# Paired attention scores, pipelined compressed attention and rope rows by DMA in a two-block float32 kernel

## The chip, the core and the metric

One core of a Trainium2 chip runs the whole program. The metric is the time of one execution on the device in microseconds. A kernel is timed in several executions, of which the median counts; one more execution is recorded by the hardware profiler, and all rows below are from it.

## What is computed

Two transformer blocks on 256 tokens of width 2048, all in float32. The first one mixes a selective-scan part (SSD) and sparse attention (NSA), then a gated feed-forward. The second mixes HGRN2 and FOX, then a feed-forward.

```python
# block 1, attention: 16 query heads of 64 in 4 key groups
q_rot = partial_rope(q, cos, sin); ks = partial_rope(ks, cos, sin); kw = partial_rope(kw, cos, sin)
k_cmp = compress_tokens(kc, ...)        # 15 compressed keys and values of 32 tokens each
o_cmp = softmax(q . k_cmp, masked) @ v_cmp
o_sel = softmax(q_rot . ks) @ vs        # n_select covers all 4 blocks: causal attention
o_win = softmax(q_rot . kw) @ vw        # the window covers all 256 tokens
o = g0 * o_cmp + g1 * o_sel + g2 * o_win
# partial_rope: of each head's 64 features, the first 8 (x1) and the next 8 (x2)
x1 * c - x2 * s, x2 * c + x1 * s
# block 2
y_a = hgrn2(q, f, i, g) @ w_up_a;  y_b = fox(q, k, v, f) @ w_up_b
x = x + rms_norm((sigmoid(g_a) * y_a + sigmoid(g_b) * y_b) @ w_o)
x = x + rms_norm((silu(h @ gate) * (h @ up)) @ w_down)
```

## The kernel before

All weights stream through once. `plan` cuts them into items (`1k`, `1q0`, `2ga3` and so on, a chunk of up to 512 output columns each) and items into units of 512 KB. SP loads unit j into one of five `raw` buffers as soon as VectorE has split unit j-5. ScalarE rounds it to `whi` (L992), VectorE takes the rest `wlo` (L1493), and TensorE multiplies three times per weight tile, whi with xhi, whi with xlo, wlo with xhi, for nearly the precision of float32. A "feat" unit is 24 matmuls of 256 moving columns, a "tok" unit 12 of 512. The units of `1mk` and `1mv` (kind "cmp", the compression weights) have only 8 matmuls. The splits run three units ahead of TensorE.

The order is written by hand. On each engine `walk` goes through the items; after each unit it calls `tick()` for short generators and then takes one step, up to its next `yield`, of a side generator: attention, compressed attention, SSD, HGRN, FOX. So the side work of the four engines moves in steps, one a unit, and a `yield` more or less on one engine shifts it by a unit against the others. Matmuls go through L411, transposes through L415.

What the change touches:
- Rope (`rope`, L652 and L1833). Six matmuls with a permutation matrix `perm` bring feature d+8 to d and back, for 2 pairs of key tiles beside `1q1` and 4 pairs of query tiles beside `1v`; VectorE multiplies by cos and sin and adds.
- Attention (`attention1`, `attend`). 24 tasks (`T1`): a task holds 4 heads for the first 128 tokens and 2 heads for the other 128, one key group `g`, one branch. Key group g lies in partitions 0 to 63 for even g and 64 to 127 for odd g, so a score matmul uses one half of the array. Task j: TensorE's scores in step j, VectorE's scaling and masking in j+1, ScalarE's exponential in j+2, TensorE's transposes of the probabilities in j+3, ScalarE's copy of them in j+4, TensorE's value products in j+4 too, VectorE's normalising `fin` in j+5. The steps lie beside `1c`, `1x0`, `1mk`, `1mv` and the start of `1x1`. Banks 4 to 7 of PSUM are handed out in turn by `take` and `give`; a `take` waits for what last read the bank.
- `taps(n)`: the convolution over four tokens of `1x0` to `1x2`, on VectorE and ScalarE, started right behind each item.
- Compressed attention (`compressed`): after the 24 tasks, one token block after the other, in one set of buffers. Its score matmuls alternate between the array's halves and two banks.
- HGRN (`hgrn`): nine levels for two groups of heads, three steps a level: score matmuls, ScalarE's exponential of differences, VectorE's predicated copy of the scores and its products `QE`, `KE` (factors) for the next level.
- `o_tiles`: transposes of the mixers' result, split into the operand of `2ua` and `2ub`. The first two pairs of tiles come right ahead of `2ua0`.
- `between_2fg0`: transposes of quads of the hidden state between the units of the first feed-forward item of block 2.

Of the kernel before, what the change touches and what calls it, by code (L numbers as in the profile page):

```python
# [6 lines left out]
P = 128  # L7
# [13 lines left out]
_CONST = [("w2k", 256), ("w2v", 128), ("ident", 128), ("U", 128), ("OS", 256), ("perm", 128), ("cm", 256), ("lev", 1024),  # L21
# [100 lines left out]
def build(nc, ins, out):  # L122
# [13 lines left out]
    with ctx:  # L136
# [80 lines left out]
        PT1 = [W_(18512, 512), W_(19024, 512)]  # L217
        RT = W_(20048, 512)
        hidT = W_(19536, 2, 256)
# [56 lines left out]
        t16a = small(16)  # L276
        sp = [small(32) for _ in range(4)]
# [20 lines left out]
        s_rope_mm, s_rope_out, s_rope = sem("s_rope_mm"), sem("s_rope_out"), sem("s_rope")  # L298
# [94 lines left out]
        def tensor(e):  # L393
# [234 lines left out]
            def hidden_T(nm):  # L628

                yield from later(2)  # L630
                kv = int(nm == "1mv")
                pb = take("hT", kv)
# [19 lines left out]
            def rope(src, n0, ntile, ready):  # L652
                for i in range(ntile // 2):
                    if i:
                        give("rope", n0 + i - 1, when=(s_rope_out, n0 + i))
                    pb = take("rope", n0 + i)
                    on.wait_ge(*ready)
                    mm(pb, C("perm"), src[:, 2 * i:2 * i + 2, :].rearrange("p a b -> p (a b)")).then_inc(s_rope_mm, 1)
                    yield
                give("rope", n0 + ntile // 2 - 1, when=(s_rope_out, n0 + ntile // 2))  # L660
                yield

            def attend(lab, n, base, outs, PM, PT, scores, values):

                for i in range(n + 5):
# [4 lines left out]
                    if 5 <= i and outs[i - 5][2]:  # L670
                        give(lab, "out", outs[i - 5][0], when=(s_fin, outs[i - 5][0] + 1))
                    if 4 <= i < n + 4:
                        j = i - 4
# [11 lines left out]
                    if i < n:  # L685
                        scores(i, take(lab, "sc", i)).then_inc(s_sc, 1)
                    yield

            def attention1():
# [3 lines left out]
                def scores(j, pb):  # L693
                    tb, hh, br, g, r0, nh, _, _ = T1[j]
                    Kn, p0 = 128 * (tb + 1), (g % 2) * 64
# [20 lines left out]
                yield from attend("a1", N1, 0, outs, PM1, PT1, scores, values)  # L716

            def compressed():
                yield
                w2k, w2v = two(C("w2k")), two(C("w2v"))  # L720
                pb = take("kc")
                on.wait_ge(s_hs, 1)
                for ht in range(2):
                    m = mm(pb[:, 0:60], w2k[:, ht, :], hid[:, 0, ht, :], start=(ht == 0), stop=(ht == 1))
                m.then_inc(s_kc, 1)
                give("kc", when=(s_kcT, 1))
                for gp in range(2):
                    pb = take("vb", gp)
                    on.wait_ge(s_hrep, 1)
                    for ht in range(2):  # L730
# [1744 lines left out]
```

## Time and profile before

| | us |
|---|---|
| median of three timed executions | 2665.29 (2656.59 to 2667.74) |
| the profiled execution | 2660.39 |
| its span in the trace | 2658.6 |
| TensorE busy | 2639.5 |
| VectorE, ScalarE busy | 1482.0, 1239.3 |
| mean granted clock of TensorE | 0.998 |

TensorE is the engine that sets the time; the others are idle for about half of it on average, but not in each stretch. A matmul's shown length reaches to its modelled end, and its successor starts before that. So the difference of two starts tells what a piece costs, and idle time is only shown where the next start lies behind the modelled end. Float32 matmuls that are not split by hand (attention, rope) show as two records each.

### The profile page before, as it was taken

The page shows a single profiled execution, that of the slowest core. Times are in us where ns is not written, and L with a number is a line of the kernel's source. Part 1 is how long each engine was busy: PE and PEld are TensorE (multiplying, and loading weights), DVE is VectorE, ACT ScalarE, POOL GpSimd, SP SyncE. Part 2 cuts the span into 40 slices and gives each one's busy share as a digit, 9 for nine tenths or more (in the row PEclk, how much of TensorE's full clock was granted, in tenths as well). Part 3 has the DMA queues.
Part 4 walks back from the last instruction along what each step waited for, and adds up shares of the span by engine and source line. Part 5 has one row for each costly group of instructions (what it writes and reads, how often), then busy time and mean ns, then how long its engine had stood idle before and what let it go on. Part 6 is the DMA issues. An engine that isn't in the chain of part 4 may idle for free.

```text
span 2658.6 us, 33234 instructions
## 1 busy us (share of the span) xinstructions
PE 2639.5 (99%) x13682; PEld 2250.4 (85%) x13682; DVE 1482.0 (56%) x1790; ACT 1239.3 (47%) x1577; POOL 0.2 (0%) x4
## 2 busy tenths in 40 slices
PE   9999999999999999999999999999999999999998
PEld 9898878888888888889889888888888888888887
DVE  6575776455445454566567654456555444555456
ACT  5465555444344434466454454444554444443443
POOL 0000000000000000000000000000000000000000
PEclk9999999999999999999999999999999999999999
DMA  8433445655555555556544445665555555655554
GB/s 300 151 105 120 151 137 193 200 188 192 192 190 189 191 194 192 188 176 218 189 156 146 154 134 182 193 226 182 184 199 195 185 194 189 194 189 191 191 193 145
DMA packets 131911, 483.64 MB, mean 182 GB/s; under 512 B 14640, under 2 KB 14896, under 8 KB 130736
## 3 DMA queue, kind: packets, MB, share of 16 engines
q1 hardware_dynamic: 131616, 481.37, 55.2%
q8 instruction: 108, 1.77, 0.3%
q14 instruction: 43, 0.35, 0.0%
q10 hardware_dynamic: 144, 0.15, 0.0%
HBM read 477.27 MB, written 4.19 MB: 181 GB/s over the span
## 4 chain that ended last, share of the span: by engine, by line
PE 97%; DVE 1%; DMA 1%; ACT 1%; issue 0%; SPq 0%; DVEq 0%; ACTq 0%
PE ps L411 95%; PE ps L415 2%; DMA h<-in_x 0%; DVE wlo L1493 0%; DMA raw<-in_w_in 0%; ACT W L992 0%; DVE xlo L1496 0%; DVE h L1496 0%; ACT whi L992 0%; DVE W L1493 0%; ACT xhi L992 0%; DVE hlo L1496 0%; DVE scr L1493 0%; SPq L2304 0%; ACT L992 0%
## 5 line engine op out<-in xcount | busy, mean ns | idle before, releaser
L1493 DVE TENSOR_TENSOR wlo<-raw,whi 128x1024 fp32r<-128x1024 f32 x886 | 1082.4, 1224 | 1031.9 <-ACT whi L992 1028.2
L992 ACT ACTIVATE whi<-raw 128x1024 fp32r<-128x1024 f32 x886 | 935.3, 1058 | 1144.9 <-PE ps L411 1133.6
L411 PE MATMUL ps<-whi,xlo 128*128 128x512 f32 x2080 | 817.6, 393 | 1.8 <-DVE xlo L1496 1.8
L411 PE MATMUL ps<-wlo,xhi 128*128 128x512 f32 x2080 | 809.9, 389 | 0.0
L411 PE MATMUL ps<-whi,xhi 128*128 128x512 f32 x2080 | 809.6, 389 | 0.0
L411 PEld LDWEIGHTS ps<-whi,xlo 128*128 128x128 f32 x2080 | 390.6, 188 | 82.4 <-issue 3.5
L411 PEld LDWEIGHTS ps<-wlo,xhi 128*128 128x128 f32 x2080 | 390.4, 188 | 81.9
L411 PEld LDWEIGHTS ps<-whi,xhi 128*128 128x128 f32 x2080 | 390.7, 188 | 80.6 <-issue 1.4
L411 PE MATMUL ps<-whi,hlo 128*128 128x512 f32 x944 | 370.1, 392 | 0.0
L411 PE MATMUL ps<-wlo,hhi 128*128 128x512 f32 x944 | 367.5, 389 | 0.0
L411 PE MATMUL ps<-whi,hhi 128*128 128x512 f32 x944 | 367.3, 389 | 0.0
L411 PE MATMUL ps<-xhi,whi 128*128 128x256 f32 (+2 forms) x992 | 284.7, 288 | 0.7 <-ACT xhi L992 0.4
L411 PE MATMUL ps<-xhi,wlo 128*128 128x256 f32 (+2 forms) x992 | 279.4, 283 | 0.6 <-DVE wlo L1493 0.6
L411 PE MATMUL ps<-xlo,whi 128*128 128x256 f32 (+2 forms) x992 | 279.3, 283 | 0.0
L411 PEld LDWEIGHTS ps<-wlo,hhi 128*128 128x128 f32 x944 | 177.2, 188 | 37.0
L411 PEld LDWEIGHTS ps<-whi,hhi 128*128 128x128 f32 x944 | 177.3, 188 | 36.6 <-issue 0.5
L411 PEld LDWEIGHTS ps<-whi,hlo 128*128 128x128 f32 x944 | 177.2, 188 | 36.4 <-issue 0.5
L411 PEld LDWEIGHTS ps<-xhi,whi 128*128 128x128 f32 (+2 forms) x992 | 187.0, 189 | 6.2 <-issue 4.6
L411 PEld LDWEIGHTS ps<-xlo,whi 128*128 128x128 f32 (+2 forms) x992 | 187.2, 189 | 1.6 <-issue 1.0
L411 PEld LDWEIGHTS ps<-xhi,wlo 128*128 128x128 f32 (+2 forms) x992 | 187.0, 189 | 1.2 <-DVE wlo L1493 0.8
L411 PE MATMUL ps<-W 128*128 128x128 f32 (+5 forms) x868 | 124.3, 294 | 7.1 <-ACT W L992 4.1
L411 PEld LDWEIGHTS ps<-W 128*128 128x128 f32 (+1 forms) x868 | 108.3, 195 | 20.3 <-issue 8.5
(128 smaller groups left out, 1023.6 us busy)
## 6 DMA issues: line engine op xcount, KB each, us to landing
raw<-in_gu SPq DMA_DIRECT2D x352, 512.0 KB, 4.1
raw<-in_w_in SPq DMA_DIRECT2D x256, 512.0 KB, 3.6
raw<-in_dn SPq DMA_DIRECT2D x176, 512.0 KB, 3.8
raw<-in_w_out SPq DMA_DIRECT2D x32, 512.0 KB, 4.0
raw<-in_w_up SPq DMA_DIRECT2D x32, 512.0 KB, 4.3
raw<-in_w_o SPq DMA_DIRECT2D x32, 512.0 KB, 3.6
raw<-in_cmp SPq DMA_DIRECT2D x8, 512.0 KB, 3.6
W<-in_wb SPq DMA_DIRECT2D x3, 1024.0 KB, 5.9
```

Of the source, the lines that this page charges most:

```text
L411: return e.matmul(o, l, r, start=start, stop=stop, skip_group_check=skip)
L415: return e.transpose(o, i, C("ident")[0:k, 0:k])
L992: return e.activation(o, i, f, **kw)
L1493: return e.tensor_tensor(o, a, b, op)
```

## The change

1. The `perm` matmuls are gone. `krot` and `qrot` are zeroed at the start by VectorE, and SP copies the 8 and 8 rows of each head crosswise into them, four DMAs for the keys and four for the queries. VectorE's `rope` starts four units later in its item and reads them.
2. Tasks of the two key groups of a half of the heads now follow each other, and the scores of tasks i and i+1 are issued together in even steps, matmul by matmul in turn in partitions 0 to 63 and 64 to 127, each group into a bank of its own. Odd steps have no scores.
3. Value products and `fin` come one step later (j+5, j+6). That holds for FOX's `attend` too.
4. `taps(0)` starts 8 units later, `hidden_T` of `1mk` 4 units later.
5. Compressed attention has two sets of buffers and works on both token blocks in neighbouring steps, 11 steps in all.
6. HGRN: TensorE starts one step later, and VectorE's predicated copy now stands in the same step as the products.
7. All of `o_tiles` lies beside `2gb3`, one pair of tiles a unit, ahead of `2ua0`.
8. In `between_2fg0` the first two quads stand one unit later.

```diff
@@ rope on VectorE, and the DMAs on SP
-            def rope(src, dst, n0, ntile, ready):
-                yield
-                for i in range(ntile // 2):
-                    t, x = 2 * i, n0 + i
-                    rv = two(RT)
-                    on.wait_ge(*ready)
-                    own.up(tt(dst[:, t:t + 2, :], src[:, t:t + 2, :], bc(C("cos"), 1, [P, 2, T]), MUL))
-                    on.wait_ge(s_rope_mm, x + 1)
-                    on.wait_ge(s_rope, x)
-                    tt(rv, two(B("rope", x)), bc(C("sin"), 1, [P, 2, T]), MUL).then_inc(s_rope_out, 1)
+            def rope(src, rot, dst, wait, ntile, landed):
+                yield from later(wait)
+                for t in range(0, ntile, 2):
+                    o, r = dst[:, t:t + 2, :], rot[:, t:t + 2, :]
+                    own.up(tt(o, src[:, t:t + 2, :], bc(C("cos"), 1, [P, 2, T]), MUL))
+                    on.wait_ge(landed, 64)
+                    own.up(tt(r, r, bc(C("sin"), 1, [P, 2, T]), MUL))
                     mine()
-                    on.wait_ge(s_rope_out, x + 1)
-                    tt(dst[:, t:t + 2, :], dst[:, t:t + 2, :], rv, ADD).then_inc(s_rope, 1)
+                    tt(o, o, r, ADD).then_inc(s_rope, 1)
                     yield
...
+            e.memset(krot, 0.0).then_inc(s_rot0, 1)
+            e.memset(qrot, 0.0).then_inc(s_rot0, 1)
...
-            walk(["1q1"], rope(kraw, kr, 0, 4, ev["1k"]))
-            walk(["1v"], rope(qf, qr, 2, 8, ev["1q1"]))
+            on.wait_ge(*ev["1k"])
+            walk(["1q1"], rope(kraw, krot, kr, 4, 4, s_krot))
+            on.wait_ge(*ev["1q1"])
+            walk(["1v"], rope(qf, qrot, qr, 4, 8, s_qrot))
...
+            def rotated(dst, src, landed):
+
+                on.wait_ge(s_rot0, 2)
+                for p0 in (0, 8, 64, 72):
+                    q0 = p0 ^ 8
+                    e.dma_start(dst[p0:p0 + 8], src[q0:q0 + 8]).then_inc(landed, 16)
...
+                elif g == end["1q0"]:
+                    on.wait_ge(*ev["1k"])
+                    rotated(krot, kraw, s_krot)
+                elif g == end["1q1"] + 1:
+                    on.wait_ge(*ev["1q1"])
+                    rotated(qrot, qf, s_qrot)
@@ attention on TensorE
-                        part = [(g, r0) for g in (2 * hh, 2 * hh + 1) for r0 in range(0, 4, nh)]
+                        part = [(g, r0) for r0 in range(0, 4, nh) for g in (2 * hh, 2 * hh + 1)]
...
-                for i in range(n + 5):
+                for i in range(n + 6):
...
-                    if 4 <= i < n + 4:
-                        j = i - 4
+                    if 5 <= i < n + 5:
+                        j = i - 5
...
-                    if i < n:
+                    if i < n and not paired:
                         scores(i, take(lab, "sc", i)).then_inc(s_sc, 1)
+                    elif i < n and i % 2 == 0:
+                        for m in scores(i, [take(lab, "sc", i), take(lab, "sc", i + 1)]):
+                            m.then_inc(s_sc, 1)
...
                     for r in range(nh):
-                        m = mm(pb[:, r * Kn:r * Kn + Kn], qr[p0:p0 + 64, (g // 2) * 4 + r0 + r, tb * 128:tb * 128 + 128],
-                               kr[p0:p0 + 64, br * 2 + g // 2, 0:Kn])
-                    return m
+                        for par in range(2):
+                            p0 = par * 64
+                            last[par] = mm(pbs[par][:, r * Kn:r * Kn + Kn], qr[p0:p0 + 64, hh * 4 + r0 + r, tb * 128:tb * 128 + 128],
+                                           kr[p0:p0 + 64, br * 2 + hh, 0:Kn])
+                    return last
@@ taps, on ScalarE and VectorE
-                    running.append(taps(n))
+                    running.append(taps(n, 8 if n == 0 else 0))
@@ between_2fg0
-                if (tb, u) == (0, 1):
+                if (tb, u) == (0, 2):
                     quads_T(0, 1)
-                elif (tb, u) == (0, 2):
+                elif (tb, u) == (0, 3):
                     quads_T(1, 1)
@@ hgrn on TensorE
+                        yield
                         if li:
                             nf += 1
                             on.wait_ge(s_fx, nf)
@@ hgrn on VectorE
                         yield
+                        yield
                         on.wait_ge(s_hm, nh + 1)
...
                         nh += 1
-                        yield
                         if m1:
@@ o_tiles, all three engines
-            walk([f"2g{x}{c}" for x in "ab" for c in range(4)], side)
-            side = o_tiles()
-            next(side)
-            walk([f"2ua{c}" for c in range(4)], side)
-            walk([f"2ub{c}" for c in range(4)])
+            walk([f"2g{x}{c}" for x in "ab" for c in range(4)][:7], side)
+            assert next(side, side) is side
+            walk(["2gb3"], o_tiles())
+            walk([f"2u{x}{c}" for x in "ab" for c in range(4)])
```

TensorE, two steps beside `1mk`, the side work between two cmp units and the first matmuls of the units around it, before. `W<-W 128x64` are value products, `cst,W 128x128` transposes, `W 128x256` scores:

```order
L411 MATMUL ps<-W 128x64 [waits s_att_probT,s_att_masked]
L411 MATMUL ps<-W 128x64 x3
L415 MATMUL ps<-cst,W 128x128 [waits s_att_prob]
L415 MATMUL ps<-cst,W 128x128 x3
L411 MATMUL ps<-W 128x256 [waits s_att_masked]
L411 MATMUL ps<-W 128x256
L411 MATMUL ps<-whi,spare 120x256 [waits s_hi]
```

The same place in the changed kernel, an even step with its pair and an odd one behind the next unit:

```order
L415 MATMUL ps<-W 128x64 x4
L419 MATMUL ps<-cst,W 128x128 [waits s_att_prob,s_att_masked]
L419 MATMUL ps<-cst,W 128x128 x3
L415 MATMUL ps<-W 128x256 [waits s_att_masked,s_att_probT]
L415 MATMUL ps<-W 128x256 x3
L415 MATMUL ps<-whi,spare 120x256 [waits s_hi]
...
L415 MATMUL ps<-W 128x64 [waits s_att_probT]
L415 MATMUL ps<-W 128x64 x3
L419 MATMUL ps<-cst,W 128x128 [waits s_att_prob,s_att_masked]
L419 MATMUL ps<-cst,W 128x128 x3
```

Four score matmuls stand where two stood, every other step; the wait for the probability copy (`s_att_probT`) stands ahead of the pair, for a bank.

VectorE, one HGRN level, before (`COPY_PREDICATED` takes the level's scores, the last products are the factors):

```order
L1493 TENSOR_TENSOR W<-W 128x16x32 x2
L1493 TENSOR_TENSOR wlo<-raw,whi 128x1024 [waits s_hi]
L2137 COPY_PREDICATED W<-cst,ps 128x512 [waits s_hgrn_read,s_hgrn_mm]
L2137 COPY_PREDICATED W<-cst,ps 128x512
L1493 TENSOR_TENSOR wlo<-raw,whi 128x1024 [waits s_hi]
L1493 TENSOR_TENSOR W<-W 128x16x32 [waits s_hgrn_exp]
```

And in the changed kernel:

```order
L1483 TENSOR_TENSOR W<-W 128x16x32 x2
L1483 TENSOR_TENSOR wlo<-raw,whi 128x1024 [waits s_hi] x2
L2127 COPY_PREDICATED W<-cst,ps 128x512 [waits s_hgrn_read,s_hgrn_mm]
L2127 COPY_PREDICATED W<-cst,ps 128x512
L1483 TENSOR_TENSOR W<-W 128x16x32 [waits s_hgrn_exp]
L1483 TENSOR_TENSOR W<-W 128x16x32
```

The copy has moved behind the second split and stands directly ahead of the products.

TensorE in `2fg0`, the first token block, before:

```order
L411 MATMUL ps<-whi,xlo 128x512 [waits s_quad_lo,s_quad_hi]
L411 MATMUL ps<-whi,xhi 128x512
L411 MATMUL ps<-wlo,xhi 128x512
L415 MATMUL ps<-cst,h 128x128 [waits s_post]
L415 MATMUL ps<-cst,h 128x128 x3
L411 MATMUL ps<-whi,xlo 128x512 [waits s_quad_lo,s_quad_hi,s_hi]
```

And in the changed kernel, the second of the two quads, which stands right ahead of the second token block (it waits for `s_xlo`):

```order
L419 MATMUL ps<-cst,h 128x128 [waits s_post]
L419 MATMUL ps<-cst,h 128x128 x3
L415 MATMUL ps<-whi,xlo 128x512 [waits s_xlo,s_xhi]
L415 MATMUL ps<-whi,xhi 128x512
L415 MATMUL ps<-wlo,xhi 128x512
```

Each of the two transposes has moved behind one more unit of six matmuls.

## Rows read from the trace of the kernel before

**Rows 1.** the page's busy times, us, share of the span, instructions
```profile
PE 2639.5 (99%) x13682; PEld 2250.4 (85%) x13682; DVE 1482.0 (56%) x1790; ACT 1239.3 (47%) x1577; POOL 0.2 (0%) x4
```

**Rows 2.** who waited for whom: us in total, times, longest
```profile
PE ps L411 <- ACT W L992: 4.1, 4, 1.4
```

**Rows 3.** stretches of the attention: us; busy and count by engine; granted clock; DMA
```profile
198.50:202.00 3.50, 3.50 (x26) 2.94 (x25) 3.39 (x9) 2.50 (x6) 0.00 (x0) 1.00 0.51 149
202.00:206.30 4.30, 2.85 (x21) 2.24 (x21) 2.86 (x8) 2.50 (x8) 0.00 (x0) 1.00 0.49 149
206.30:213.10 6.80, 6.80 (x28) 5.63 (x26) 5.78 (x13) 3.40 (x7) 0.00 (x0) 0.50 0.23 80
```

**Rows 4.** timeline of TensorE at a rope matmul: start, length, engine, what
```profile
57.43 0.28 PE L411 MATMUL ps<-xhi,wlo 128*128 128x256 f32 x1
...
57.55 1.02 PE L411 MATMUL ps<-W,cst 128*128 128x512 f32 x2
...
58.52 0.28 PE L411 MATMUL ps<-xlo,whi 128*128 128x256 f32 x1
```

**Rows 5.** SP's own waits, and its weight loads, from the page
```profile
SPq L2295 <- DVE wlo L1493: 2307.4, 880, 19.0
...
raw<-in_w_in SPq DMA_DIRECT2D x256, 512.0 KB, 3.6
```

**Rows 6.** timeline of VectorE, start of the program
```profile
0.88 0.27 DVE L2249 MEMSET W<- 128x256 f32 x1
...
5.77 1.23 DVE L1493 TENSOR_TENSOR wlo<-raw,whi 128x1024 fp32r<-128x1024 f32 x1 [4.62 <-ACT whi L992]
```

**Rows 7.** timeline of TensorE: attention steps with one score task, and without
```profile
184.32 1.00 PE L411 MATMUL ps<-W 128*128 128x64 f32 x8
...
185.15 0.61 PE L415 MATMUL ps<-cst,W 128*128 128x128 f32 x4
...
189.72 1.00 PE L411 MATMUL ps<-W 128*128 128x64 f32 x8
...
240.32 1.00 PE L411 MATMUL ps<-W 128*128 128x64 f32 x8
...
244.46 1.00 PE L411 MATMUL ps<-W 128*128 128x64 f32 x8
```

**Rows 8.** timeline of TensorE, a task of the first token block
```profile
113.20 1.16 PE L411 MATMUL ps<-W 64*128 64x128 f32 x8
114.29 0.39 PE L411 MATMUL ps<-xhi,whi 128*128 128x256 f32 x1
```

**Rows 9.** timeline of TensorE, scores of the compressed attention
```profile
273.73 1.96 PE L411 MATMUL ps<-W 64*128 64x15 f32 x32
275.62 0.39 PE L411 MATMUL ps<-xhi,whi 128*128 128x256 f32 x1
```

**Rows 10.** timeline of VectorE, a row of the taps
```profile
199.27 1.51 DVE L1496 SCALAR_TENSOR_TENSOR W<-W,cst 128x255 f32<-128x255 f32 x3
```

**Rows 11.** timeline of TensorE at the start of 2ua0
```profile
1733.62 0.39 PE L411 MATMUL ps<-whi,xlo 128*128 128x512 f32 x1
...
1734.30 1.03 PE L415 MATMUL ps<-cst,scr 128*128 128x128 f32 x8
...
1737.16 0.47 PE L411 MATMUL ps<-whi,xlo 128*128 128x512 f32 x1 [1.83 <-DVE xlo L1496]
```

**Rows 12.** timelines of TensorE and VectorE at the third hgrn level
```profile
1350.26 0.49 PE L411 MATMUL ps<-W 128*128 128x128 f32 x2 [1.70 <-DVE W L1493]
...
1340.93 1.34 DVE L2137 COPY_PREDICATED W<-cst,ps 128x512 f32<-128x512 int32 x2
```

**Rows 13.** timelines of TensorE, ScalarE and VectorE in 2fg0
```profile
1927.68 1.09 PE L415 MATMUL ps<-cst,h 128*128 128x128 f32 x8 [0.97 <-DVE h L1496]
...
1924.00 1.14 ACT L992 ACTIVATE xhi<-ps,cst 128x128 fp32r<-128x128 f32 x4 [0.68 <-PE ps L415]
...
1925.18 1.13 DVE L1496 SCALAR_TENSOR_TENSOR xlo<-ps,cst,xhi 128x128 fp32r<-128x128 f32 x4 [0.70 <-ACT xhi L992]
```

More of the change, by code:

```diff
@@ L217, in build @@
         PT1 = [W_(18512, 512), W_(19024, 512)]
+        SXC = [SX1[0][:, 0:240], SX1[0][:, 256:496]]
         RT = W_(20048, 512)
+        krot = W_(6144, 4, T)
+        qrot = W_(7168, 8, T)
         hidT = W_(19536, 2, 256)
@@ L276, in build @@
         t16a = small(16)
+        t16c = [t16a, small(16)]
         sp = [small(32) for _ in range(4)]
@@ L628, in hidden_T @@
             def hidden_T(nm):
-                yield from later(2)
                 kv = int(nm == "1mv")
+                yield from later(2 if kv else 6)
                 pb = take("hT", kv)
@@ L650, in start_side, with attend @@
                 spread()
-            def rope(src, n0, ntile, ready):
-                for i in range(ntile // 2):
-                    if i:
-                        give("rope", n0 + i - 1, when=(s_rope_out, n0 + i))
-                    pb = take("rope", n0 + i)
-                    on.wait_ge(*ready)
-                    mm(pb, C("perm"), src[:, 2 * i:2 * i + 2, :].rearrange("p a b -> p (a b)")).then_inc(s_rope_mm, 1)
-                    yield
-                give("rope", n0 + ntile // 2 - 1, when=(s_rope_out, n0 + ntile // 2))
-                yield
-            def attend(lab, n, base, outs, PM, PT, scores, values):
-                for i in range(n + 5):
+            def attend(lab, n, base, outs, PM, PT, scores, values, paired=False):
+                for i in range(n + 6):
                     if 4 <= i < n + 4:
@@ L715, in attention1 @@
                     k += t[7]
-                yield from attend("a1", N1, 0, outs, PM1, PT1, scores, values)
+                yield from attend("a1", N1, 0, outs, PM1, PT1, scores, values, paired=True)
             def compressed():
-                yield
                 w2k, w2v = two(C("w2k")), two(C("w2v"))
[L721 to L730, printed above, removed]
-                        m = mm(pb[0:120, 0:64], hrep[:, ht, gp * 120:gp * 120 + 120], w2v[:, ht, :], start=(ht == 0), stop=(ht == 1))
-                    m.then_inc(s_vb, 1)
-                    give("vb", gp, when=(s_bd, gp + 1))
-                yield
@@ L1159, in start_side @@
             def start_side():
[L1160 to L1166 removed]
+                yield from later(8)
+                for i in range(8):
+                    tb, c = i // 4, i % 4
+                    on.wait_ge(s_x, 32)
+                    square("A", tb, c, h[:, tb, c * 512:c * 512 + 512])
+                    if i in (2, 5):
+                        yield
                 root("A")
@@ L1192, in hidden @@
             def hidden(kv):
-                yield from later(2)
+                yield from later(2 if kv else 6)
                 on.wait_ge(s_hT, kv + 1)
@@ L1202, in flat_hi, with taps @@
                     yield
-            def taps(n):
-                yield
+            def taps(n, wait):
+                yield from later(wait + 1)
                 for j in range(4):
@@ L1214, in attend @@
                 n = len(tasks)
-                for i in range(n + 5):
+                for i in range(n + 6):
                     if 4 <= i < n + 4:
@@ L1590, in after @@
                     features(nm, CT, 0, banks)
-                    running.append(taps(n))
+                    running.append(taps(n, 8 if n == 0 else 0))
                 elif nm[:3] == "1oa":
@@ L1869, in flatten, with taps @@
                     yield
-            def taps(n):
-                yield
-                yield
+            def taps(n, wait):
+                yield from later(wait + 2)
                 cw = C("convw")
```

294 lines of the change are left out of this document (142 added, 152 removed).

## The prediction

> **What bounds the kernel now.** I read the page's busy times first: TensorE is busy for 2639.5 of 2658.6 us [rows 1], so only TensorE's own work, its few waits and its clock can move the end. The list of who waited for whom, cut to TensorE, puts four waits for ScalarE's copies at 4.1 us together [rows 2]. The table by stretches shows one stretch, 206.3 to 213.1 us, in which the granted clock was 0.50, the lower of its two levels (1.2 of 2.4 GHz), and just before it a stretch of 4.30 us in which TensorE was busy for 2.85 [rows 3]. All of this lies in the sparse and windowed attention of block 1. The timelines then give what each piece costs. A figure of the timeline's second column can't be used as a price, since matmuls overlap; prices are differences of starts, those of the next work included.
>
> **The change, part by part.** The profiled execution took 2660.4 us (span 2658.6), which is 4.9 below the median of the three timed runs; the sum is made against it.
>
> 1. Rope matmuls. The matmul with `perm` starts at 57.55 and the second main matmul behind it at 58.52, where the two main ones before stand 0.12 apart [rows 4]: 58.52 - 57.55 - 0.12 = 0.85 us. There are six: 5.1 us gone. What replaces them are 8 small DMAs on SP's queue, each group of four behind a wait for the eviction of `1k` or `1q1`. SP spends 2307 us waiting in front of 880 weight loads, 2.6 us each [rows 5], so the issues fit there. No row shows a transfer that small; one of 512 KB lands in 3.6 us [rows 5], and four one after the other would be 14.4. VectorE asks for them four units later. If they were late VectorE would hold its splits back, and these run three units ahead of TensorE, so I take nothing, with up to 3 us as the bad end. The zeroing of `krot` and `qrot` stands at VectorE's start: 256 columns took 0.27 us, so 3072 are some 2.6 to 3.2 us, ending before 4.4; VectorE's first split starts at 5.77 [rows 6]. Nothing, and no gain.
>
> 2. Scores in both halves. A step of the attention with one score task lasts from 184.32 to 189.72, 5.40 us, and one without scores from 240.32 to 244.46, 4.14 us [rows 7]: one task costs 1.26 us. A task of the first token block is eight narrower records that delay the next main matmul from 113.20 to 114.29 [rows 8]; by the same subtraction it costs 1.27. 24 tasks: 30.2 us. Afterwards 12 pairs. How far do halves overlap? The compressed scores alternate halves already: 32 records hold the next main matmul off by 1.89 us [rows 9], against 1.09 for eight in one half. The value products, eight records in 0.83 us [rows 7], give 0.104 each for loads in a row, so the edge of a block is 1.09 - 0.83 = 0.26 and an alternating record costs (1.89 - 0.26) / 32 = 0.051, just half. Those records move 15 columns; the paired ones move 128 and 256, which no row shows alternating. Bounds: full overlap makes a pair cost what one task did, 12 x 1.26 = 15.1 gained; no overlap saves the edges alone, which are some 1.26 - 0.83 = 0.43 a block, 12 x 0.43 = 5.2. I take 14.8, near the full end, since the nearest row overlaps fully and a little is left for the stagger.
> The Trainium skill, page "TensorE: Matmul & The Clock Gate", section "Part 3: Packing small matmuls", measured four row tiles of 512 columns at 3.07 times one, not four. By that (an estimate from that page) a pair would stream about 1.3 times as long as one task, and this term would be near 11.7 instead of 14.8.
>
> 3. Waits inside the attention. The longest, 1.4 us [rows 2], lies in the stretch from 202.0 to 206.3 [rows 3]. Its cause: VectorE had 3.39 us of work in the step of 3.50 before it [rows 3], of which the taps of `1x0` are 1.51 [rows 10]; it fell behind, the exponentials and the probability copy behind it too, and the value products wait for that copy of the same step. The change does two things to it: `taps(0)` starts 8 units later, beside units that last 2.88 us instead of about 1, and the value products come one step after the copy. A short unit's main work is 3.50 less the block's 5.40 - 24 x 0.12 = 2.52, about 1.0 us. With the pairs, steps of short units are 3.5 with scores and 2.2 without, 2.9 in the mean, while VectorE then has 3.39 - 1.51 = 1.9 us in one and ScalarE 2.5 [rows 3]. I take the four waits as gone: 4.1, and 0.16 for each since idle is counted only from the modelled end (0.28 after a start, where the next would start after 0.12 [rows 4]): 4.7.
>
> 4. The clock. 6.8 us at half speed [rows 3] cost 3.4. It fell right behind the sparsest stretch; with the waits gone I take it as gone: 3.4, with 0 as the other end, and as a rival below a loss.
>
> 5. Compressed attention over steps. The four waits of [rows 2] are all that TensorE has for ScalarE's copies, and they lie before it; its matmuls stay the same. Zero. The selective-scan part starts one unit later and ends inside `1oa` still: zero.
>
> 6. Tiles for `2ua0`. TensorE waits 1.83 us for the split of the first tiles [rows 11]; now tile k is made right behind unit k/2 of `2gb3`, which was the last reader of that operand tile. The wait goes, with its 0.16: 2.0.
>
> 7. hgrn. TensorE waits 1.70 us for the factors, until 1350.26 [rows 12]. The change gives it a unit more, 2.72 us (three main matmuls take 0.68 [rows 11], a unit has twelve), but moves VectorE's predicated copy, 1.34 us [rows 12], from a time in which VectorE has nothing else to do to right in front of the factor products. Factors then stand at 1350.26 + 1.34 = 1351.6; TensorE arrives at 1350.26 - 1.86 + 2.72 = 1351.1. 0.5 of the 1.86 stays, 1.4 is gained.
>
> 8. `2fg0`. The two quad transposes slide by one unit of 1.36 us. At the place that waits now, 1927.68, TensorE wants VectorE's `post(2, .)` [rows 13]. VectorE does these after the residues of quad (1,1), from 1925.18, which wait for ScalarE, from 1924.00, which waits for the transposes that slide [rows 13]. So they end 1.4 later, and the wait of 0.97 grows to 2.4: 1.4 lost. Nothing hides it; the first quad did not wait before.
>
> Sum: -5.1 - 14.8 - 4.7 - 3.4 - 2.0 - 1.4 + 1.4 = -30.0. 2660.4 - 30.0 = 2630.4 for an execution like the profiled one. The four executions known average 2662.4, the median of three is 2665.3; I add 2 and forecast **2632**.
>
> **The rivals.**
> (a) The halves don't overlap for wide moving operands, the change not doing what it says: term 2 is 5.2, time 2632 + 9.6 = 2642. For it: no row shows it. Against: the 15-column rows, whose weight loads overlap fully. 0.10.
> (b) They overlap in part, each pair 0.26 longer: 12 x 0.26 = 3.1, time 2635. This is the case that the Trainium skill's figure of 3.07 speaks for. 0.10.
> (c) The wait moves and stays. On even steps all four spare banks are in use, so a pair's scores wait for ScalarE's probability copy and VectorE's masking of the same step. TensorE gets there about 1.0 + 1.3 = 2.3 us into a short step; ScalarE's whole step is 2.50 [rows 3], of which the exponentials, half of it or so, come after the copy. So there is about 1 us of slack; if VectorE or ScalarE are later than that in the short steps, the 4.7 and the 3.4 come back: 2640. 0.12.
> (d) Slower. A step without scores has less for TensorE, and pairs do in 1.26 what took 2.5; if that makes the clock fall at the first short units and stay low, each us of wall time at 1.2 GHz costs half. The gain of 30 is gone at 60 us of it; the whole attention, 114 us from 113.20 [rows 8] to some 227 before and 114 - 15 - 8 = 91 after, would cost 91 more: 2723. For it: the drop came in just these short units. Against: the two stretches before it ran at 1.00, one with a long wait in it [rows 3]. 0.03.
> (e) A stall that I don't see, up to 10 us: 2642. 0.05.
>
> **How the numbers follow.** Forecast 0.60, rivals as given. Executions before spread over 11 us, some 5 either way; the forecast's own case is 2624 to 2640. (b) lies in it, (a), (c) and (e) reach 2647 with the spread. I take **2623 to 2645**, which leaves out (d) and the upper part of (a), (c) and (e). A change of under 0.5%, 13 us, can't be told from none here: the border is 2652. Faster 0.92, same 0.05 (parts of (c) and (e) together with (a)), slower 0.03, which is (d).
>
> **What would show it.** Twelve blocks of paired scores with starts a few ns apart, a step with scores no longer than 5.4 us, a step without 4.15; no matmul with `perm`; granted clock 1.00 at 190 to 215 us; TensorE's waits for ScalarE gone; no wait in front of `2ua0`; about 0.3 us at the third hgrn level; a wait of about 2.4 us for `h` in `2fg0`. If the paired blocks last 2 us, (a) holds. If TensorE waits in front of scores, (c). Wrong altogether would be a TensorE waiting on `s_rope` or on its splits after the rope, or a long stretch at 0.50.

## The result, and the profile after

The changed kernel took **2636.12 us** (median of four executions, 2635.18 to 2636.91), the kernel before 2662.45 (four, 2656.59 to 2667.74). The ratio is 0.9899, with a 95% interval of 0.9875 to 0.9923: 1.0% faster, and inside the stated range. The profiled execution took 2636.87 with a span of 2635.1, 23.5 us less than the 2658.6 of before, where the sum of the prediction had 30.0. So the sign and most of the size held; 6.5 us are to be explained.

The page's busy times of the changed kernel, which answer to [rows 1]:

```profile
PE 2617.9 (99%) x13670; PEld 2238.4 (85%) x13670; DVE 1483.2 (56%) x1792; ACT 1238.9 (47%) x1577; POOL 0.2 (0%) x4
```

Who waited for whom, TensorE's rows (us in total, times, longest), which answer to [rows 2]:

```profile
PE ps L419 <- DVE h L1486: 2.2, 1, 2.2
PE ps L415 <- DVE sm L1886: 1.9, 3, 1.1
PE ps L419 <- DVE sm L1886: 1.4, 1, 1.4
PE ps L415 <- DVE W L2237: 1.2, 1, 1.2
PE ps L419 <- DVE scr L1483: 1.2, 1, 1.2
PE ps L415 <- ACT W L989: 0.9, 1, 0.9
PE ps L419 <- ACT W L989: 0.2, 1, 0.2
```

The 1.2 us for `W` stands at the very start of the program, in both kernels. None of the waits of [rows 2] for the copy ahead of value products is left. But TensorE waits in new places: for VectorE's masks (1.9 and 1.4 us), once for a probability copy (0.9), for `scr` (1.2) and for `h` (2.2, before 0.97 in [rows 13]). TensorE's timeline, one row of each kind: a pair of the first token block, the block behind it, the two places with the longest new waits, a step with a pair and the next one without, the transposes behind the compressed attention, and `2fg0`:

```profile
107.00 1.16 PE L415 MATMUL ps<-W 64*128 64x128 f32 x16
...
108.09 0.39 PE L415 MATMUL ps<-xhi,whi 128*128 128x256 f32 x1
...
122.20 0.63 PE L419 MATMUL ps<-cst,W 128*128 128x128 f32 x4 [0.17 <-ACT W L989]
...
123.73 1.16 PE L415 MATMUL ps<-W 64*128 64x128 f32 x16 [0.91 <-ACT W L989]
...
139.75 0.66 PE L419 MATMUL ps<-cst,W 128*128 128x128 f32 x4 [1.38 <-DVE sm L1886]
...
143.10 1.00 PE L415 MATMUL ps<-W 128*128 128x64 f32 x8
...
148.52 1.00 PE L415 MATMUL ps<-W 128*128 128x64 f32 x8
...
152.66 1.00 PE L415 MATMUL ps<-W 128*128 128x64 f32 x8
...
194.28 1.13 PE L415 MATMUL ps<-W 64*128 64x256 f32 x8 [1.08 <-DVE sm L1886]
...
272.70 0.63 PE L419 MATMUL ps<-cst,scr 128*128 128x128 f32 x4 [1.19 <-DVE scr L1483]
...
1902.47 1.09 PE L419 MATMUL ps<-cst,h 128*128 128x128 f32 x8 [2.22 <-DVE h L1486]
```

The pair of 16 records at 107.00 delays the next main matmul to 108.09, as one task of eight did in [rows 8]. The step from 143.10 to 148.52 lasts 5.42 us and holds two score tasks, the next one, to 152.66, lasts 4.14: the step lengths of [rows 7]. The stretches of the attention, and the one behind the wait in `2fg0` (us; busy and count by engine; granted clock; DMA share; GB/s), for [rows 3]:

```profile
107.00:224.00 117.00, 112.41 (x963) 106.24 (x963) 81.88 (x245) 80.75 (x199) 0.00 (x0) 1.00 0.39 127
1903.60:1907.00 3.40, 3.40 (x9) 2.62 (x8) 2.85 (x6) 2.08 (x5) 0.00 (x0) 0.51 0.29 89
```

The clock stays at its upper level through the whole attention. It falls to the lower one for 3.4 us at 1903.6, right behind the wait of 2.22. Of the four executions two had spans of 2635.1 and two of 2633.4 and 2633.6, and the difference of 1.7 is what 3.4 us at half clock cost. Only the profiled execution has a trace, so that the two shorter ones lack this stretch is read from their spans; 2633.4 is taken below as the kernel without it.

Lining up the same main matmul in both traces gives what each part was worth, in us:

| step of the prediction | predicted | measured |
|---|---|---|
| 1 rope matmuls | -5.1 | -5.3 |
| 2 pairs of scores | -14.8 | -15.1 |
| 3 waits of the attention | -4.7 | -4.7, and +5.4 of new ones |
| 4 half clock in it | -3.4 | -3.4 |
| 5 compressed attention | 0 | +1.35 at its end |
| 6 tiles for `2ua0` | -2.0 | -2.0 |
| 7 hgrn | -1.4 | -2.0 |
| 8 `2fg0` | +1.4 | +1.25, and +1.7 by the clock |
| not in it: sums of squares at the start | | -0.9 |

Lining up gives -17.8 for the waits, the pairs and the clock of the attention together. The step lengths, the idle times and the granted clock divide it: -15.1, -4.7 and -3.4 are read from them, and the 5.4 of new waits is the rest.

### The profile page after: what moved, and what is told of

Its sections match the earlier page's. It is cut to its first block, busy times and chain, and to the rows that moved or that the text cites. A ratio compares the mean times of both kernels' runs of the same rounds, so it can differ in the third digit from the quotient of the medians.

```text
span 2635.1 us, 33219 instructions
## 1 busy us (share of the span) xinstructions
PE 2617.9 (99%) x13670; PEld 2238.4 (85%) x13670; DVE 1483.2 (56%) x1792; ACT 1238.9 (47%) x1577; POOL 0.2 (0%) x4
## 4 chain that ended last, share of the span: by engine, by line
PE 98%; DVE 1%; ACT 1%; issue 0%; DVEq 0%
PE ps L415 96%; PE ps L419 2%; ACT W L989 0%; DVE W L1483 0%; DVE W L1886 0%; DVE scr L1483 0%; DVE wlo L1483 0%; DVE h L1486 0%; ACT whi L989 0%; ACT L989 0%; ACT xhi L989 0%; DVE xlo L1486 0%; ACT sm L989 0%; DVEq L2339 0%; DVE sm L1483 0%
## 5 line engine op out<-in xcount | busy, mean ns | idle before, releaser
L415 PE MATMUL ps<-W 128*128 128x128 f32 (+5 forms) x868 | 109.0, 291 | 4.0 <-DVE sm L1886 1.9
L415 PEld LDWEIGHTS ps<-W 128*128 128x128 f32 (+1 forms) x868 | 98.8, 194 | 13.0 <-issue 9.4
```

What stands on the lines that cost most here:

```text
L415: return e.matmul(o, l, r, start=start, stop=stop, skip_group_check=skip)
```

## Experiments

All edits are made to the changed kernel unless another is named. A cost is again a difference of starts: from the last main matmul ahead of a block to the first behind it, less the cadence of 0.12.

### Does the order of the halves matter, and do the halves?

One half after the other (`seq_halves`):

```diff
-                    for r in range(nh):
-                        for par in range(2):
+                    for par in range(2):
+                        for r in range(nh):
                             p0 = par * 64
```

> The changed kernel, with one edit: a pair of score tasks is issued one half after the other (all matmuls of partitions 0 to 63, then all of 64 to 127) instead of in turn. Theory 1, the gain of the pairs is overlap of matmuls that stand next to each other in different halves: a pair costs what 16 records in a row do, some 1.28 + 8 x 0.105 = 2.1 us instead of 1.28, and twelve of them make the span about 10 us longer, 2645. Theory 2, the gain comes from having half as many blocks and the overlap is only small: each pair costs some 0.3 us more, the span is about 2638. Theory 3, the two halves run side by side in whatever order they are issued: no change, 2635.

Measured: span 2635.1, with no half clock at 1904; median 2636.93 (2636.77 to 2638.49), 0.8 above the changed kernel. Against the changed kernel's 2633.4 without half clock the span is 1.7 longer. TensorE's timeline of `seq_halves`, the first pair and a pair of 256 columns with the main matmul behind each:

```profile
106.88 1.71 PE L415 MATMUL ps<-W 64*128 64x128 f32 x16
...
108.52 0.39 PE L415 MATMUL ps<-xhi,whi 128*128 128x256 f32 x1
...
145.98 1.14 PE L415 MATMUL ps<-W 64*128 64x256 f32 x8
...
147.05 0.38 PE L415 MATMUL ps<-xhi,whi 128*128 128x256 f32 x1
```

The pair of 256 columns takes 1.07 us to the next main matmul, the same as in turn (144.48 to 145.54). So for the eight pairs of the second token block theory 3 holds. The pair of 128 columns takes 1.64 instead of 1.09: there eight records stand in each half, and 0.55 are lost, four times, of which one falls into a wait that is there anyway. The single records in the trace show why: the eight records of 256 columns start in four pairs, 14 ns apart within a pair (145.983 and 145.997, 146.303 and 146.317, and so on), though all four of the first half were issued ahead of the second half's; with eight a half, four start alone before the first pair (107.427 and 107.433), and five alone at the end. So the second half's first record started beside the fifth of the first half, ahead of three that were issued before it. What keeps it from starting earlier was not looked into.

Both tasks in the same half (`same_half`; the scores of odd key groups are left out, those of even ones computed twice):

```diff
-                            p0 = par * 64
+                            p0 = 0
```

> The changed kernel in which both tasks of a pair read partitions 0 to 63, so the scores of odd key groups are left out and those of even ones computed twice; order, banks and shapes are the same. Theory 1, only different halves of the array overlap: 16 records of 128 columns or 8 of 256 take twice what one task did, the block some 0.84 us more than the 1.28 of the changed kernel, about 10 us over twelve pairs, less what falls into waits that are there anyway (under 2.5), 2641 to 2645 as span. Theory 2, it is the alternation of two banks that lets them overlap: no change.

TensorE's timeline at the first pair:

```profile
107.05 2.05 PE L415 MATMUL ps<-W 64*128 64x128 f32 x16
...
109.03 0.39 PE L415 MATMUL ps<-xhi,whi 128*128 128x256 f32 x1
```

The pair now takes 1.98 to the next main matmul instead of 1.09; those of 256 columns cost 2.12 instead of 1.27. The span is 2644.3, 9.2 more than the changed kernel's. Theory 1: it is the halves, not the banks. Together: a pair in two halves costs what one task cost, within 0.02 us. The Trainium skill, page "TensorE: Matmul & The Clock Gate", section "Part 3: Packing small matmuls", has 3.07 for four row tiles; no run here has four. For two halves the estimate that the prediction drew from it, 11.7 us, does not hold: the pairs gave 15.1. The same section says that matmuls start and end in strict order of issue; the starts in `seq_halves` were not in that order.

### What caused the old waits and the half clock?

Value products and normalising back by a step (`values_back`):

```diff
-                    if 5 <= i < n + 5:
-                        j = i - 5
+                    if 4 <= i < n + 4:
+                        j = i - 4
...
-                    if 6 <= i:
-                        fin(i - 6)
+                    if 5 <= i < n + 5:
+                        fin(i - 5)
```

> The changed kernel with the value products and the normalising one step earlier again (steps j+4 and j+5), in the attention of both blocks. Theory 1, value products in the step of ScalarE's copy were what TensorE waited for: waits ahead of 128x64 value products of about 0.9 us come back, three or more of them beside the short units, 3 to 5 us in all, and a stretch at half clock with them (up to 3.4 more). Theory 2, the pairs and the later taps had already given ScalarE the time: no such wait, the span within 1 us of 2635.

Span 2642.4, 7.3 more: theory 1. TensorE's timeline at two of its waits, and the stretch at half clock:

```profile
123.81 1.08 PE L415 MATMUL ps<-W 128*128 128x64 f32 x8 [1.71 <-ACT W L989]
...
127.08 2.08 PE L415 MATMUL ps<-W 64*128 64x128 f32 x16 [1.65 <-DVE sm L1886]
```

```profile
125.10:131.90 6.80, 5.15 (x32) 4.60 (x30) 3.89 (x23) 3.18 (x12) 0.00 (x0) 0.50 0.51 154
```

TensorE's waits for ScalarE's copies come back as 4.5 us in four, and 6.8 us at half clock behind the first of them. Three of the four are the old 0.85 to 0.96 us, at 196, 210 and 220 us. So it is the move by a step that removed them, and not the pairs.

`taps(0)` without the delay of 8 units (`taps_now`), on ScalarE and VectorE alike:

```diff
-                    running.append(taps(n, 8 if n == 0 else 0))
+                    running.append(taps(n, 0))
```

> The changed kernel with taps(0) started right behind 1x0, as before the change. Theory 1, VectorE's load by the taps makes everything behind it late beside the short units: TensorE waits 1.5 us or more in one place there, the total of its waits between 175 and 205 us rises from 2.4 to 5 or more, and the clock falls to 0.5 behind it. Theory 2, the step that the value products were moved takes up the lateness: the total rises by less than 1 us and the clock stays.

TensorE's timeline at its longest wait, and the stretch at half clock:

```profile
199.09 2.08 PE L415 MATMUL ps<-W 64*128 64x256 f32 x8 [2.51 <-DVE sm L1886]
```

```profile
198.50:205.30 6.80, 6.21 (x29) 5.48 (x29) 4.98 (x14) 2.15 (x5) 0.00 (x0) 0.50 0.39 149
```

Span 2640.9. The waits between 175 and 214 us are 6.3 us instead of 2.1, the longest 2.51 for a mask, and the clock is at half for 6.8 us from 198.5, which the changed kernel does not have: 4.1 and 3.4, less the 1.7 that it did not lose at 1904. Theory 1.

The kernel before with only the delayed taps (`before_taps8`), again on both engines:

```diff
-                    running.append(taps(n))
+                    running.append(taps(n, 8 if n == 0 else 0))
...
-            def taps(n):
-                yield
+            def taps(n, wait):
+                yield from later(wait + 1)
...
```

> The kernel before with one edit: taps(0) on ScalarE and VectorE starts 8 units later. Theory 1, the taps are the cause of the wait at 205 us and of the half clock behind it: both are gone, the span is 4 to 6 us shorter than 2658.6, and the executions spread by less than the 11 us of the kernel before, because that spread is the length of the stretch at half clock. Theory 2, the wait comes from the value products standing in the step of the copy: it stays, and the time is that of before within 1 us.

TensorE's timeline at the place of [rows 3], and its waits for ScalarE's copies:

```profile
205.01 1.10 PE L411 MATMUL ps<-W 128*128 128x64 f32 x8 [0.96 <-ACT W L992]
```

```profile
PE ps L411 <- ACT W L992: 3.6, 4, 1.0
```

The wait at 205 us is 0.96 instead of 1.45 and the other three stay: of the wait, theory 2 is right, the copy stands in the same step, and the taps made 0.5 of it. But the clock did not fall behind it there. In the profiled execution it fell for 3.4 us each behind later waits, at 224.0 and 1736.1, so its span of 2658.3 is no shorter. Over twelve executions the median is 2656.54, ratio 0.9969 (0.9952 to 0.9986): eight had spans of 2653.9 to 2655.7, four 2658.3 to 2668.8. So theory 1's smaller spread did not come, it was 15 us; but two thirds of the executions were in the short group, where the kernel before has a sixth: of 42 executions of it that were timed beside these experiments only seven had 2655.0 to 2655.8 (mean clock 0.999); four had 2658.3 to 2658.6 (0.998), thirteen 2663.4 to 2666.0 (0.995 to 0.996) and eighteen 2669.2 to 2673.6 (0.992 to 0.993). So its spread goes with the clock, and the profiled execution with its 6.8 us at half clock was one of the better ones. By spans, the change gains 2655.5 - 2633.4 = 22.1 us against executions of the fastest kind, and 36 to 40 against the eighteen of the slowest.

### What are the new waits?

Both masks of a pair in the odd step (`masks_together`), with a third buffer, and normalising in even steps:

```diff
-                    if 1 <= i < n + 1:
-                        j = i - 1
+                    for j in ((i - 1, i) if i % 2 and i < n else ()) if paired else ((i - 1,) if 1 <= i < n + 1 else ()):
...
+                    if paired and 5 <= i < n + 5:
+                        fin(i - 5)
...
```

> The changed kernel in which VectorE masks both tasks of a pair in the odd step behind the scores, into one of three buffers instead of two, and normalises in even steps (j+5). Theory 1, pairs of scores wait for a bank that the second task of the pair before still occupies until VectorE masks it in the same step: the waits ahead of scores at about 181, 194 and 200 us (0.56, 1.08, 0.24) and of transposes at 140 us (1.38) are gone, the span is 3.5 to 4 us shorter than the changed kernel's. Theory 2, ScalarE is what is late, since it frees the transposes' bank by its copy in the same step too: the waits stay within 30% of these, gain under 1 us. Theory 3, two masks in one short step overload VectorE (1.4 to 1.7 us more in steps of 2.2): new waits in front of the splits or transposes, and the span is longer.

TensorE's timeline at 123 us and between 190 and 200 us:

```profile
123.08 0.63 PE L419 MATMUL ps<-cst,W 128*128 128x128 f32 x4 [1.02 <-ACT W L989]
...
194.51 1.13 PE L415 MATMUL ps<-W 64*128 64x256 f32 x8
...
198.48 0.66 PE L419 MATMUL ps<-cst,W 128*128 128x128 f32 x4 [0.85 <-DVE sm L1885]
```

The scores no longer wait (theory 1), but transposes in odd steps now do: 0.85 at 198.48, with 0.32 and 0.37 in two others, and the wait at 140 stays (1.38). They take a bank of the pair whose mask stands in that very step, behind VectorE's split: theory 3, in its place though not by overload. There is overload too, at 112.4 to 114.1 us, where the eight masks of the first pair stand in a row. They hold back a small product of VectorE that ScalarE waits for, 1.33 us instead of 0.48. ScalarE's later work, the copy ahead of the transposes at 123.08 included, comes later by as much, and that wait is 1.02 instead of 0.17. Span 2634.4 without half clock at 1904, 1.0 longer than 2633.4, and 0.9 of it is this one place; median 2637.02 (2636.22 to 2637.79).

Both masks already in the even step, behind the scores (`masks_early`), with four buffers:

```diff
-                    if 1 <= i < n + 1:
-                        j = i - 1
+                    if paired and 6 <= i:
+                        fin(i - 6)
+                    for j in ((i, i + 1) if i % 2 == 0 and i < n else ()) if paired else ((i - 1,) if 1 <= i < n + 1 else ()):
...
```

> The changed kernel in which VectorE masks both tasks of a pair at the end of the even step in which their scores are issued, into one of four buffers. Theory 1, all waits of the attention but those behind ScalarE's table loads come from banks whose mask stands behind VectorE's work of the next step: the waits at 181, 194 and 200 us (0.56, 1.08, 0.24) and at 140 us (1.38) go, and no new one comes in front of the transposes, unlike with masks in the odd step; the one at 122 to 124 us (0.17 and 0.91) stays, since it waits for ScalarE. The span is 3.5 us (3 to 4.3) below the changed kernel's 2633.4 without or 2635.1 with the half clock at 1904 us. Theory 2, VectorE waiting for scores holds back its splits: waits ahead of main matmuls between 110 and 205 us, gain under 1 us or a loss.

TensorE's longest waits in the whole kernel, the start left out:

```profile
PE ps L419 <- DVE h L1486: 2.2, 1, 2.2
PE ps L419 <- DVE scr L1483: 1.2, 1, 1.2
PE ps L415 <- ACT W L989: 0.9, 1, 0.9
```

Theory 1, to the number: only 0.91 of ScalarE's at 123.46 is left of the waits over 0.2 us in the attention, span 2629.5, 3.9 less than 2633.4. Median 2632.34 (2631.28 to 2633.17).

ScalarE's logarithm, with its table loads, seven units later (`ln_later`):

```diff
-                yield from softplus(1, 32, 1)
+                yield from softplus(1, 32, 1, 7)
...
```

> The changed kernel in which ScalarE's logarithm of the softplus (with the table loads that it needs, 1.28 us each, before and behind it) comes seven units later. Theory 1, these loads are what makes the probability copy late at 122 to 124 us: the waits of 0.17 and 0.91 us there are gone, and where the loads stand now, beside units of 2.9 us, they cost at most 0.4: 1.0 to 1.3 us gained up to 130 us, in the whole 0.6 to 1.3. Theory 2, it is the first exponentials themselves (1.6 us a task) that are late: the wait stays above 0.6.

ScalarE's timeline of the changed kernel shows the loads; the fence below is TensorE's in `ln_later`, at the place to which they moved:

```profile
117.49 1.28 ACT L989 ACT_TABLE_LOAD   x1
...
119.11 1.28 ACT L989 ACT_TABLE_LOAD   x1
```

```profile
163.27 1.10 PE L415 MATMUL ps<-W 64*128 64x256 f32 x7 [0.69 <-ACT W L989]
```

The waits of 0.17 and 0.91 are gone (1.3 us up to 130 us), and 0.9 comes back at 163 and just before. Theory 1 as to the cause, but in the whole 0.35 us gained, less than its range.

### The places outside the attention

An empty step of TensorE ahead of the transposes of the attention's result (`later_T`):

```diff
             def attention_T():
+                yield
                 for k in range(0, 8, 2):
```

> The changed kernel with one empty step on TensorE between the compressed attention and the transposes of the attention's result. Theory 1, pipelining the compressed attention left VectorE's last additions only one short distance ahead of these transposes: the wait of 1.19 us at 272.7 us is gone, 1.35 us gained. Theory 2, VectorE is late by more than a step or the next stage becomes late instead: less than 0.5 us.

The wait for `scr` is gone, nothing else moved: the main matmuls from 440 us on stand 1.3 us earlier against those ahead of it. Theory 1 (one execution, span 2633.6, half clock at 1902 included).

The quad transposes back at their places (`quads_back`):

```diff
-                if (tb, u) == (0, 2):
+                if (tb, u) == (0, 1):
                     quads_T(0, 1)
-                elif (tb, u) == (0, 3):
+                elif (tb, u) == (0, 2):
```

> The changed kernel with the first two quad transposes of the first feed-forward item of block 2 back at their places of before. Theory 1, moving them by a unit made the wait there 2.2 instead of 1.0 us, and the stretch at half clock behind it (3.4 us, a loss of 1.7) follows from the longer wait: the wait is 1.0 us, no half clock behind it, the span 2635.1 - 1.3 - 1.7 = 2632.1. Theory 2, the wait has another cause, such as the post step of VectorE: it stays above 2 us and the span is 2633 to 2635.

TensorE's timeline at that wait:

```profile
1901.10 1.09 PE L419 MATMUL ps<-cst,h 128*128 128x128 f32 x8 [0.96 <-DVE h L1486]
```

Span 2632.1 in all four executions (2632.1 to 2632.2), as theory 1 had it; median 2633.92, 2.2 below the changed kernel. The wait is 0.96, the trace has no half clock behind it, and by their spans the other three executions have none either.

ScalarE's sums of squares at the start as before (`start_back`):

```diff
-                yield from later(8)
-                for i in range(8):
+                yield from later(6)
+                for tb in range(2):
+                    for c in range(4):
...
```

> The changed kernel with ScalarE's eight sums of squares at the start grouped two a step from the seventh step on, as in the kernel before, instead of spread over three steps from the ninth. Theory 1, this small edit is what removed TensorE's wait of 0.57 us for a split at 34 us: the wait is back and the span 0.7 to 0.8 us longer up to there. Theory 2, the wait varies by itself or by the loads from memory: none.

TensorE's timeline at 34 us:

```profile
34.17 0.39 PE L415 MATMUL ps<-xhi,wlo 128*128 128x256 f32 x1 [0.64 <-DVE wlo L1483]
```

The wait is back, and from there to the end the main matmuls stand 0.9 us later. Theory 1. This edit is a part of the change that the description ahead of the prediction leaves out.

### Together

`best2`: `masks_early`, `quads_back`, `later_T` and `ln_later` in one kernel.

> Four edits on top of the changed kernel, all measured alone before: masks in the even step with four buffers, the two quad transposes of block 2 back at their old places, an empty step of TensorE ahead of the transposes of the attention's result, and ScalarE's logarithm seven units later. Theory 1, the waits are independent, so the gains add: from the 2629.5 us of the run with early masks 1.35 for the wait at 269 us, 1.25 for the one at 1899 us and 0.1 to 1.2 for the one at 123 us, a span of 2625.7 to 2626.9 with no half clock before the end in any execution, so that all executions agree within 0.5 us; some 9 us (0.35%) faster than the changed kernel. Theory 2, removing one wait makes the next engine late (as with the logarithm alone, where 0.9 of 1.3 us came back at 163 us): a span above 2628.

All of TensorE's waits in its list:

```profile
PE ps L415 <- DVE W L2239: 1.2, 1, 1.2
PE ps L419 <- DVE h L1487: 1.0, 1, 1.0
PE ps L419 <- DVE scr L1484: 0.6, 1, 0.6
```

Theory 1: median **2628.40** (six executions, 2628.20 to 2628.46), 7.7 us below the changed kernel, ratio to the kernel before 0.9865 (0.9843 to 0.9887). From `masks_early` to here 2.9 us, of which 1.35 and 1.25 are the two single edits, so the later logarithm gave 0.3; a wait of 0.56 for the normalising is what it left. TensorE waits for nothing else over 0.12 us but at the start (1.2) and in `2fg0` (1.0).

## Why the prediction was right, and where it was off

- **Steps 1, 2 and 6** were right to 0.3 us. For step 2 the nearest row, compressed scores of 15 columns [rows 9], told the truth for 128 and 256 columns as well; rivals (a) and (b) fell. That a full overlap had been priced at 14.8 rather than 15.1 is the small rest that was left for the stagger, and there is none.
- **Step 3, "I take the four waits as gone".** They went, by the causes that were named, as `values_back` and `taps_now` show. But the taps made only 0.5 of the longest wait; the rest of it and the other three came from the copy in the same step (`before_taps8`). But the step failed in what is late next. That was described in rival (c), "a pair's scores wait for ScalarE's probability copy and VectorE's masking of the same step", and dismissed with a slack of about 1 us worked out from a mean step. The slack isn't that of the mean step: at 194 us VectorE's mask stood behind its split, this behind ScalarE's split at 191.13, this behind the eviction of `1mk` at 189.39, which waits for that item's last matmul (the rows below). At 140 us the eviction of `1c` stands ahead of the mask in the same way. Cost 3.8 us there and at the other masks. At 122 to 124 us it is ScalarE, with 2.56 us of table loads: 1.3 us, which no step had looked for, and some 0.3 in places too small to name. Of (c)'s 8.1 us, 5.4 came back as waits, none as clock.
- **Step 4** was right in the profiled execution, but mis-sized for the median: it took the 6.8 us of one execution for the typical stretch. Other executions of the kernel before had spans up to 19 us above the fastest, at a lower mean clock. The 2 us that I added to come from the profiled execution to the mean of before (2662.5, not 2662.4) should have been left out: the changed kernel lies within 1.7 us. That it brought the forecast nearer to the result is chance.
- **Step 5, "Zero"**, looked at the waits inside the compressed attention and not at who comes behind it. The distance on TensorE, from the last values to the transposes of the result, is the same (284.88 to 292.22 before, 264.17 to 271.35 now). But VectorE now does the additions of both token blocks in a row with one split between them, behind the eviction of `1x1`, from 265.65 to 272.5, where before it had the last ones done at 288.9, 3.3 us ahead of the transposes. 1.35 us, as `later_T` shows.
- **Step 7** left 0.5 us of a wait that went completely. The factors were to be 1.34 us later because of the copy; but VectorE's split ahead of the copy, which waits for ScalarE and stood at 1347.78 before, now stands at 1323.36, with TensorE's matmuls 22.6 earlier: 1.8 us earlier against them. I had taken its start as fixed.
- **Step 8** was right in its mechanism: 0.97 became 2.22, predicted 2.4. It stopped at the wait and did not ask what the clock does behind a wait of that length: another 1.7 us in two of four executions.
- Rival (d), a clock that falls in the short steps and stays low, did not come: 1.00 throughout. Rope's DMAs were never waited for.

ScalarE's and VectorE's timelines of the changed kernel ahead of the wait at 194 us, for step 3:

```profile
189.39 0.87 ACT L989 ACTIVATE W<-ps 120x256 f32<-120x256 f32 x2 [1.90 <-PE ps L415]
...
191.13 1.05 ACT L989 ACTIVATE whi<-raw 128x1024 fp32r<-128x1024 f32 x1
...
192.22 1.23 DVE L1483 TENSOR_TENSOR wlo<-raw,whi 128x1024 fp32r<-128x1024 f32 x1 [2.78 <-ACT whi L989]
193.36 0.42 DVE L1886 CUSTOM_DVE_ANT_0 W<-ps,cst 128x256 f32<-128x256 f32 x1
```

VectorE was idle for 2.78 us ahead of that split: it was late without being loaded. And VectorE's split at the third hgrn level, before and changed, for step 7:

```profile
1347.78 1.23 DVE L1493 TENSOR_TENSOR wlo<-raw,whi 128x1024 fp32r<-128x1024 f32 x1 [5.51 <-ACT whi L992]
...
1323.36 1.23 DVE L1483 TENSOR_TENSOR wlo<-raw,whi 128x1024 fp32r<-128x1024 f32 x1 [4.96 <-ACT whi L989]
```

The Trainium skill, page "ScalarE: Activation LUTs", section "What ACT_TABLE_LOAD costs", gives 1283 ns for a load; this case's rows agree (1.28).

## What to carry to other kernels

Where a few buffers are handed round between engines, take for each `take` the place in the order of the engine that frees the buffer, not its mean load: a short operation that stands behind another engine's long one is as late as that one, and moving it ahead (`masks_early`) gave 3.9 us where piling two masks up in the next step (`masks_together`) lost 1.0. Small score matmuls that fill half of the array's rows should be issued in pairs from both halves. And a wait is priced with what the clock does behind it, which takes several executions to see, not one.

## What was not expected of the hardware

- Matmuls of the other half start ahead of matmuls that were issued before them: with four records a half issued one half after the other, the halves started in pairs 14 ns apart and took the time of one.
- The clock fell to its lower level behind some waits and not others, in the same kernel. Ten traces have the wait of 2.2 us in `2fg0`: it fell behind it in six (the changed kernel, `values_back`, `same_half`, `ln_later`, `later_T`, `start_back`) and not in four (`seq_halves`, `taps_now`, `masks_together`, `masks_early`). The four traces with 0.96 or 0.97 there (the kernel before, `before_taps8`, `quads_back`, `best2`) have no fall, and the spans of the other executions of `quads_back` and `best2` show none. But it fell at 224.0 us in `before_taps8` with only waits of 0.85 and 0.96 ahead of it. A stretch at the lower level with matmuls in it lasted 3.4 or 6.8 us. What decides was not found.
- Of the kernel before, 35 of 42 executions had a lower mean clock and 3 to 19 us more than the fastest; of the changed kernel none of four had more than 1.7.
